# Levels three to five of the block inverse on quarters of the TensorE array

## The chip, the cores and the metric

The kernel runs on one core of a Trainium2 chip. The metric is the device time of one execution in microseconds; of several executions the median counts. TensorE (PE in the profile) multiplies matrices: a weight load (PEld) puts the stationary operand into its 128 x 128 array, and a matmul streams the moving operand past it into PSUM. A matmul whose stationary operand is smaller than the array needs only a part of it; which part follows from the partitions that its operands come from (rows) and the partitions of PSUM that it writes (columns). The trace gives this form as rows*columns, such as 128*64. VectorE (DVE), ScalarE (ACT) and GpSimd (POOL) do the elementwise work, SyncE (SP) starts most of the transfers.

## What is computed

One step of a small hybrid decoder: a first layer with windowed attention and a gated delta rule side by side, a second with a Conformer convolution. The part around the change is the delta rule, which is computed in chunks; it asks for the inverse of a unit lower triangular matrix in every chunk and head:

```python
def gated_delta_rule(q, k, v, g, beta, s0):
    ...
    lower = jnp.tril(jnp.einsum('...id,...jd->...ij', kb, kc) * decay, -1)
    a_mat = lower + jnp.eye(c, dtype=f32)
    rhs = jnp.concatenate([vc * bc[..., None], kb * jnp.exp(gcum)[..., None]], axis=-1)
    sol = lax.linalg.triangular_solve(a_mat, rhs, left_side=True, lower=True, unit_diagonal=True)
    ...
    s_fin, o = lax.scan(step, s0.astype(f32), (u, w, attn, qg, kg, g_last))
```

There are eight heads and 512 prompt tokens. The kernel takes chunks of 128 tokens, so a head has four matrices of 128 x 128 to invert. The rest is projections: 132 weight tiles of 2048 x 128 against 576 tokens (512 of the prompt, 64 sampled), 2048 channels each.

## The kernel before

**The projections.** Every weight tile and the activations are split in two parts (`w_hi`, `w_lo`, `act_hi`, `act_lo`), and `proj` (L596) does one eighth of a tile with twelve matmuls: two blocks of 128 channels, three products each, two halves of 288 tokens. The eighths are the clock of the kernel: every engine has a list by eighths (slots), written out by hand, and TensorE takes its queue strictly in the order in which it is written.

**A head in 32 slots.** `head_unit` runs through four weight tiles, 32 slots, while it does the delta rule of the head before: `PE_PLAN`, `DVE_PLAN`, `ACT_PLAN` and `POOL_PLAN` say which step stands in which slot. Steps wait for each other through counters (`pe_h`, `dve_h`, `act_h`, `pool_h`).

**The inverse.** `solve_blocks` inverts the 8 x 8 blocks on the diagonal on VectorE (L1787 is its shuffle). Then levels 3 to 6 double the size of the inverted blocks. `POOL` masks the level's part of the matrix into `mtl` (step `L{l}`). TensorE multiplies it by the inverse so far (step `a{l}`, L817, for level 6 L820), ScalarE copies the product out of PSUM (`A{l}`), TensorE multiplies the transposed inverse by that copy (step `x{l}`, L830, for level 6 L839), and VectorE subtracts the result from the inverse (`X{l}`). As the 128 x 128 matrix falls into two blocks of 64 up to level 5, the inverse is kept compactly in `x_d`: 64 columns for each chunk, its lower-right block on the upper 64 partitions and its upper-left block on the lower 64 (`lower` and `upper` are these halves of the partitions, `diagonal` is the pair of them). The transposed inverse `xt` is kept at full width, 128 x 128 for each chunk, with zeros outside the two blocks. Levels 3 and 4 make it anew by transposing `x_d` (`T{l}`, L1858; the first is made by `Xt`, and `X` transposes it into `x_d`, L1839). Level 5 updates both `x_d` and `xt`, with eight more matmuls for the second (L835).

**How the level steps use the array.** In `a` and `x` of levels 3 to 5 there are two matmuls for each of four chunks, one for each half. Each takes all 128 rows (its operands come from all partitions, half of one of them being zeros) and 64 columns. Every fp32 matmul stands in the trace as two passes, so eight matmuls are 16 rows of the trace (x16). All four chunks' results lie in one bank of PSUM: bank 1 for `a`, bank 2 for `x`, bank 3 for the second product of level 5.

Of the kernel before, what the change touches and what calls it, by code (L numbers as in the profile page):

```python
# [20 lines left out]
P = 128  # L21
# [3 lines left out]
SEQ = 512  # L25
NC = SEQ // P
NS = NB * NT
# [8 lines left out]
LEVELS, FIRST = 7, 3  # L36
# [179 lines left out]
def hybrid_step(nc, x, wt, w_ab, const, param, dn_prev, state_in, k_cache, v_cache, cf_prev,  # L216
# [3 lines left out]
    with ExitStack() as ctx:  # L220
# [57 lines left out]
        o_tok = cut(SEQ).rearrange("p (c t) -> p c t", t=P)  # L278
        a1 = cut(SEQ).rearrange("p (c t) -> p c t", t=P)
        st = cut(P)  # L280
# [15 lines left out]
        lower, upper = slice(0, HP2), slice(HP2, P)  # L296
        diagonal = (lower, upper)
        kq_sq = fa[:, 3584:4608].rearrange("p (c t) -> p c t", t=P)
        o_sq = fa[:, 4096:4608].rearrange("p (c t) -> p c t", t=P)
# [284 lines left out]
        def _(pe):  # L584
# [203 lines left out]
            def head_step(it, kb, name):  # L788
# [21 lines left out]
                elif name[0] == "a":  # L810
# [3 lines left out]
                    if l < LEVELS - 1:  # L814
                        for c in range(NC):
                            for h_ in diagonal:
                                ins = pe.matmul(gp[h_, 1, cd(c)], mtl[l % 2][:, c, h_], x_d[:, c, :], start=True, stop=True)  # L817
                    else:
                        for c, out in ((0, upper), (2, lower), (1, upper), (3, lower)):
                            ins = pe.matmul(gp[out, 1, cd(c)], mtl[l % 2][:, c, upper], x_d[:, c, :], start=True, stop=True)  # L820
                elif name[0] == "x":
# [4 lines left out]
                    if l < LEVELS - 1:  # L826
                        for c in range(NC):
                            for h_ in diagonal:
                                a_ = a1_d[:, c, :] if l in IN_BLOCKS else a1[:, c, h_]
                                ins = pe.matmul(half_blocks(gp[h_, 2, cd(c)], l, 0), xt[:, c, h_], half_blocks(a_, l, 0),  # L830
                                                start=True, stop=True)
                        if l not in IN_BLOCKS:
                            for c in range(NC):
                                for h_ in diagonal:
                                    ins = pe.matmul(half_blocks(gp[h_, 3, cd(c)], l, 1), a1[:, c, h_],  # L835
                                                    half_blocks(xt[:, c, h_], l, 1), start=True, stop=True)
                    else:
                        for c, out in ((0, lower), (2, upper), (1, lower), (3, upper)):
                            ins = pe.matmul(gp[out, 3, cd(c)], a1_d[:, c, :], xt[:, c, upper], start=True, stop=True)  # L839
                elif name == "o_chan":  # L840
# [279 lines left out]
        def _(act):  # L1120
# [69 lines left out]
            def head_act(it, kb, name):  # L1190
# [11 lines left out]
                elif name[0] == "A":  # L1202
                    l = int(name[1])
                    act.wait_ge(pe_h.sem, pe_h.at(f"a{l}", it))
                    a_ = gp[:, 1, 0:NC * HP2].rearrange("p (c t) -> p c t", t=HP2)
                    if l in IN_BLOCKS:
                        ins = copy(a1_d, a_)
                    elif l < LEVELS - 1:
                        for h_ in diagonal:
                            ins = copy(a1[h_, :, h_], a_[h_])  # L1210
                    else:
                        copy(a1_d[upper, 0:2], a_[upper, 0:2])
                        ins = copy(a1_d[upper, 2:NC], a_[lower, 2:NC])
# [315 lines left out]
        def _(dve):  # L1529
# [264 lines left out]
            def head_dve(it, kb, name):  # L1794
# [34 lines left out]
                elif name == "Xt":  # L1829
                    dve.wait_ge(dve_h.sem, dve_h.at("solve", it))  # L1830
                    ins = tt(xt.rearrange("p c (b j) -> p c b j", j=BLOCK), blocks_wide(z_h, P),
                             blocks_mask(z_h, C_BLK + P, P), MUL)
                elif name == "X":
                    if isinstance(it, int) and it == 0:
                        for h_, other in (diagonal, diagonal[::-1]):
                            dve.memset(a1[h_, :, other], 0.0)
                    dve.wait_ge(dve_h.sem, dve_h.at("Xt", it))
                    for h_ in diagonal:
                        ins = dve.transpose(x_d[h_], xt[h_, :, h_])  # L1839
                elif name[0] == "X":  # L1840
# [3 lines left out]
                    if l < LEVELS - 1:  # L1844
                        part = half_blocks(x_d.rearrange("p c t -> p (c t)"), l, 0)
                        ins = tt(part, part, half_blocks(gp[:, 2, 0:NC * HP2], l, 0), SUB)
                        if l not in IN_BLOCKS:
                            b_ = 1 << l
                            for h_ in diagonal:
                                part = xt[h_, :, h_][:, :, b_:2 * b_]  # L1850
                                ins = tt(part, part, new(3)[h_, :, b_:2 * b_], SUB)
                    else:
                        ts(xt[lower, 0:2, upper], new(3)[lower, 0:2], -1.0)
                        ins = ts(xt[lower, 2:NC, upper], new(3)[upper, 2:NC], -1.0)
                elif name[0] == "T":
                    dve.wait_ge(dve_h.sem, dve_h.at(f"X{name[1]}", it))
                    for h_ in diagonal:
                        ins = dve.transpose(xt[h_, :, h_], x_d[h_])  # L1858
                elif name[0:2] == "vp":
# [946 lines left out]
```

## Time and profile before

| | us |
|---|---|
| median of 3 runs | 1935.72 |
| lowest and highest | 1934.87, 1937.52 |
| the profiled execution | 1932.56 |
| its span, first to last instruction | 1930.7 |
| busy: PE, DVE, ACT, POOL | 1905.5, 1244.3, 713.8, 658.9 |
| granted TensorE clock, mean | 0.997 of full |

The profile's page gives for each engine its busy time, for 40 slices of the span the busy share of each engine, the waits and the chain of work that ended last. The chain that ended last is 88% TensorE, 76% on the one line of `proj`. The timeline gives the instructions of an engine in order of time, those of one kind merged, with their start, how long the merged ones took together, and their count.

### The profile page before, as it was taken

How to read it: one execution, taken by the hardware profiler on the slowest of the kernel's cores; microseconds unless marked ns; L12 is line 12 of the kernel's file. 1: busy time of each engine (PE TensorE's matmuls, PEld its weight loads, DVE VectorE, ACT ScalarE, POOL GpSimd, SP SyncE). 2: the span in 40 equal slices, each digit the busy share in tenths (PEclk: the TensorE clock that was granted, in tenths of full speed). 3: DMA queues.
4: the chain of work that ended last, by engine and by line, in shares of the span. 5: the costliest groups of instructions: out<-in, count | busy, mean ns of one | idle time of the engine just before them, and what ended most of it. 6: DMA issues, size and time to landing. Idle time of an engine off the chain costs nothing.

```text
span 1930.7 us, 37255 instructions
## 1 busy us (share of the span) xinstructions
PE 1905.5 (99%) x15516; PEld 1857.2 (96%) x15516; DVE 1244.3 (64%) x2515; ACT 713.8 (37%) x1303; POOL 658.9 (34%) x652
## 2 busy tenths in 40 slices
PE   7999999999999999999999999999999999999997
PEld 6999999999999898899999999999999999999997
DVE  6767766776654556745332689999999755473334
ACT  5322222232222135533222455555565433342220
POOL 0222322232222220003110468888888750031110
PEclk9999999999999999999999999999999999999998
DMA  6322222222223542123434334333333222233333
GB/s 203 94 73 72 73 68 73 72 74 68 68 73 117 167 161 61 55 69 124 132 118 127 93 100 98 98 82 91 97 99 89 79 88 66 88 96 121 105 107 119
DMA packets 78361, 186.31 MB, mean 96 GB/s; under 512 B 26944, under 2 KB 32000, under 8 KB 77944
## 3 DMA queue, kind: packets, MB, share of 16 engines
q1 hardware_dynamic: 70272, 166.42, 29.0%
q0 software_dynamic: 4176, 11.74, 1.9%
q10 hardware_dynamic: 3744, 5.77, 0.8%
q8 instruction: 122, 2.00, 0.4%
q14 instruction: 47, 0.39, 0.1%
HBM read 164.82 MB, written 19.08 MB: 95 GB/s over the span
## 4 chain that ended last, share of the span: by engine, by line
PE 88%; DVE 6%; POOL 2%; issue 2%; DMA 1%; ACT 1%; SPq 0%; POOLq 0%; DVEq 0%; ACTq 0%
PE acc L596 76%; POOL arena L2350 2%; PE acc L674 2%; DVE full L1542 1%; DVE w_lo L1539 1%; DVE act_lo L1539 1%; DVE gp L1542 1%; PE gp L817 1%; PE gp L830 1%; PE gp L808 1%; PE gp L965 1%; PE gp L978 1%; PE gp L986 1%; DMA w_raw<-wt 1%; DVE arena L1539 1%
## 5 line engine op out<-in xcount | busy, mean ns | idle before, releaser
L596 PE MATMUL acc<-act_hi,w_hi 128*128 128x288 f32 x3936 | 864.6, 301 | 3.4 <-DVE w_lo L1539 3.1
L596 PE MATMUL acc<-act_hi,w_lo 128*128 128x288 f32 x3936 | 841.8, 295 | 0.0
L596 PE MATMUL acc<-act_lo,w_hi 128*128 128x288 f32 x3936 | 841.0, 295 | 0.0
L596 PEld LDWEIGHTS acc<-act_hi,w_hi 128*128 128x128 f32 x3936 | 629.8, 189 | 20.7 <-issue 12.1
L596 PEld LDWEIGHTS acc<-act_hi,w_lo 128*128 128x128 f32 x3936 | 633.1, 189 | 0.0
L596 PEld LDWEIGHTS acc<-act_lo,w_hi 128*128 128x128 f32 x3936 | 632.2, 188 | 0.0
L2350 POOL TENSOR_TENSOR arena<-arena 128x512 f32<-128x512 f32 (+1 forms) x268 | 377.6, 1409 | 338.4 <-ACT arena L1385 278.3
L1122 ACT ACTIVATE w_hi<-w_raw 128x1024 fp32r<-128x1024 f32 x264 | 277.3, 1058 | 419.8 <-PE acc L596 294.4
L1539 DVE TENSOR_TENSOR w_lo<-w_raw,w_hi 128x1024 fp32r<-128x1024 f32 x264 | 373.4, 1434 | 40.8 <-ACT w_hi L1122 39.9
L1542 DVE SCALAR_TENSOR_TENSOR gp<-arena,par,gp 128x64 f32<-128x64 f32 (+1 forms) x688 | 248.0, 441 | 0.0
L1122 ACT ACTIVATE arena<-arena,par 128x512 f32<-128x512 f32 x240 | 165.2, 720 | 103.8 <-POOL arena L2350 91.9
L1539 DVE TENSOR_TENSOR full<-acc,arena 128x576 f32<-128x576 f32 (+3 forms) x52 | 36.8, 708 | 229.8 <-PE acc L596 211.9
L2350 POOL TENSOR_TENSOR small<-small 128x4 f32<-128x4 f32 (+3 forms) x95 | 55.0, 584 | 189.6 <-DVE small L1547 73.5
L2350 POOL TENSOR_TENSOR arena<-arena,cst 128x24 f32<-128x24 f32 (+4 forms) x93 | 30.2, 342 | 254.9 <-DVE arena L1539 127.9
L2350 POOL TENSOR_TENSOR full<-full,cst 128x512 f32<-128x512 f32 x40 | 69.4, 1745 | 79.8 <-DVE full L1839 46.2
L2350 POOL TENSOR_TENSOR act_lo<-full,act_hi 128x576 fp32r<-128x576 f32 (+1 forms) x32 | 43.9, 1392 | 145.5 <-ACT act_hi L1122 145.4
L1542 DVE SCALAR_TENSOR_TENSOR arena<-arena,small 128x512 f32<-128x512 f32 (+2 forms) x145 | 74.4, 559 | 0.5
L1542 DVE SCALAR_TENSOR_TENSOR arena<-arena,acc 128x576 f32<-128x576 f32 x24 | 18.0, 750 | 81.2 <-ACT arena L1478 74.2
L1122 ACT ACTIVATE full<-gp 128x256 f32<-128x256 f32 (+1 forms) x48 | 16.5, 343 | 142.8 <-PE gp L817 115.0
L1122 ACT ACTIVATE arena<-gp,small 128x128 f32<-128x128 f32 x28 | 10.3, 367 | 151.6 <-PE gp L855 107.0
L1122 ACT ACTIVATE arena<-gp 128x512 f32<-128x512 f32 (+4 forms) x50 | 26.3, 552 | 98.4 <-PE gp L978 36.3
L1539 DVE TENSOR_TENSOR full<-full,gp 128x576 f32<-128x576 f32 (+2 forms) x72 | 32.7, 488 | 31.8 <-PE gp L835 22.7
(270 smaller groups left out, 1687.0 us busy)
## 6 DMA issues: line engine op xcount, KB each, us to landing
w_raw<-wt SPq DMA_DIRECT2D x264, 512.0 KB, 4.0
full<-x SPq DMA_DIRECT2D x8, 576.0 KB, 9.1
arena<-x SPq DMA_DIRECT2D x16, 288.0 KB, 3.6
arena<-x_scratch SPq DMA_DIRECT2D x16, 288.0 KB, 2.9
x_scratch<-full ACTq DMA_DIRECT2D x14, 288.0 KB, 4.0
arena<-state_in SPq DMA_DIRECT2D x6, 512.0 KB, 5.1
out_sdn<-arena POOLq DMA_DIRECT2D x6, 512.0 KB, 3.1
out_y<-full SPq DMA_DIRECT2D x16, 160.0 KB, 1.9
```

What stands on the lines that cost most here:

```text
L596: ins = pe.matmul(acc[:, s, i, 0:HALF], w[:, s, wk], a[:, k, i * HALF:(i + 1) * HALF], start=(k == 0 and j == 0), stop=(k == KT - 1 and j ...
L674: ins = pe.matmul(acc[:, s, a, 0:part_width(a, n >= N_OUT1)], w[:, s, wk], x_[:, k, part(a, n >= N_OUT1)], start=(k == 0 and j == 0), stop ...
L808: ins = pe.matmul(gp[:, 2 + c // 2, (c % 2) * 256:(c % 2) * 256 + 256], kt[:, ck(c)], kqv[kb][:, 0:2, ck(c)], start=True, stop=True)
L817: ins = pe.matmul(gp[h_, 1, cd(c)], mtl[l % 2][:, c, h_], x_d[:, c, :], start=True, stop=True)
L830: ins = pe.matmul(half_blocks(gp[h_, 2, cd(c)], l, 0), xt[:, c, h_], half_blocks(a_, l, 0), start=True, stop=True)
L965: ins = pe.matmul(gp[:, q, j * 256 + w * P:j * 256 + (w + 1) * P], full[rows, 4 * r + 2 * jj + j, blk(c):blk(c) + P], kv[rows, 2 * r, blk( ...
L978: ins = pe.transpose(gp[:, 2 + w, g * P:(g + 1) * P], prob[u % 2][:, g, w * P:(w + 1) * P], ident)
L986: ins = pe.matmul(gp[64 * q:64 * q + 64, 2, 0:256], v_tok[:, c - 1 + w, r, 64 * q:64 * q + 64], probT[:, w, 2 * q:2 * q + 2, :], start=(w ...
L1122: return act.activation(out, in_, ACT.Copy, scale=scale)
L1539: return dve.tensor_tensor(out, a, b, op)
L1542: return dve.scalar_tensor_tensor(out=out, in0=a, scalar=scalar, in1=b, op0=op0, op1=op1)
L2350: return pool.tensor_tensor(out, a, b, op)
```

## The change

The transposed inverse of levels 3 to 5 becomes compact too: a new tile `xt_d` of 64 columns for each chunk takes the place of `a1`. For chunks 0 and 1 (`straight`) it lies on the same half of the partitions as `x_d`, for chunks 2 and 3 (`crossed`) on the other half; `turned_home` gives the half. All matmuls of levels 3 to 5 take operands from 64 partitions. The results of chunks 2 and 3 go to a second bank, and the chunks are taken in the order 0, 2, 1, 3. The copy `A{l}` reads two banks, and is one instruction for level 5 as well. On VectorE `Xt`, `X` and `T{l}` are three instructions each (chunks 0 and 1, then each half of chunks 2 and 3), and `X5` writes the full-width `xt` with four subtractions, from the second product of level 5, which is now computed at full width (64 columns). Level 6 works on the full `xt` as before, with 64 rows instead of 128 in its second step.

```diff
         o_tok = cut(SEQ).rearrange("p (c t) -> p c t", t=P)
-        a1 = cut(SEQ).rearrange("p (c t) -> p c t", t=P)
+        xt_d = cut(SEQ)[:, 0:SEQ // 2].rearrange("p (c t) -> p c t", t=HP2)
         st = cut(P)
...
         diagonal = (lower, upper)
+        straight, crossed = slice(0, NC // 2), slice(NC // 2, NC)
+
+        def turned_home(half, c):
+
+            return half if c < NC // 2 else diagonal[half == lower]
         kq_sq = fa[:, 3584:4608].rearrange("p (c t) -> p c t", t=P)
...
                     if l < LEVELS - 1:
-                        for c in range(NC):
+                        for c in (0, 2, 1, 3):
                             for h_ in diagonal:
-                                ins = pe.matmul(gp[h_, 1, cd(c)], mtl[l % 2][:, c, h_], x_d[:, c, :], start=True, stop=True)
+                                ins = pe.matmul(gp[turned_home(h_, c), c // 2, cd(c % 2)], mtl[l % 2][h_, c, h_], x_d[h_, c, :],
+                                                start=True, stop=True)
                     else:
...
                     if l < LEVELS - 1:
-                        for c in range(NC):
+                        for c in (0, 2, 1, 3):
                             for h_ in diagonal:
-                                a_ = a1_d[:, c, :] if l in IN_BLOCKS else a1[:, c, h_]
-                                ins = pe.matmul(half_blocks(gp[h_, 2, cd(c)], l, 0), xt[:, c, h_], half_blocks(a_, l, 0),
-                                                start=True, stop=True)
+                                r_ = turned_home(h_, c)
+                                ins = pe.matmul(half_blocks(gp[h_, 2 + c // 2, cd(c % 2)], l, 0), xt_d[r_, c, :],
+                                                half_blocks(a1_d[r_, c, :], l, 0), start=True, stop=True)
                         if l not in IN_BLOCKS:
                             for c in range(NC):
-                                for h_ in diagonal:
-                                    ins = pe.matmul(half_blocks(gp[h_, 3, cd(c)], l, 1), a1[:, c, h_],
-                                                    half_blocks(xt[:, c, h_], l, 1), start=True, stop=True)
+                                for r_ in diagonal:
+                                    ins = pe.matmul(gp[r_, 2, cd(4 + c)], a1_d[r_, c, :], xt_d[r_, c, :], start=True, stop=True)
                     else:
                         for c, out in ((0, lower), (2, upper), (1, lower), (3, upper)):
-                            ins = pe.matmul(gp[out, 3, cd(c)], a1_d[:, c, :], xt[:, c, upper], start=True, stop=True)
+                            ins = pe.matmul(gp[out, 3, cd(c)], a1_d[upper, c, :], xt[upper, c, upper], start=True, stop=True)
                 elif name == "o_chan":
...
                     a_ = gp[:, 1, 0:NC * HP2].rearrange("p (c t) -> p c t", t=HP2)
-                    if l in IN_BLOCKS:
-                        ins = copy(a1_d, a_)
-                    elif l < LEVELS - 1:
-                        for h_ in diagonal:
-                            ins = copy(a1[h_, :, h_], a_[h_])
+                    if l < LEVELS - 1:
+                        ins = copy(a1_d.rearrange("p (b c) t -> p b (c t)", b=2), gp[:, 0:2, 0:P])
                     else:
...
                     dve.wait_ge(dve_h.sem, dve_h.at("solve", it))
-                    ins = tt(xt.rearrange("p c (b j) -> p c b j", j=BLOCK), blocks_wide(z_h, P),
-                             blocks_mask(z_h, C_BLK + P, P), MUL)
+                    wide = xt_d.rearrange("p c (b j) -> p c b j", j=BLOCK)
+                    for h_, chunks in ((slice(0, P), straight), (lower, crossed), (upper, crossed)):
+                        z = z_h[h_, chunks]
+                        ins = tt(wide[h_ if chunks == straight else diagonal[h_ == lower], chunks], blocks_wide(z, HP2),
+                                 blocks_mask(z, C_BLKM, NS)[h_], MUL)
                 elif name == "X":
                     if isinstance(it, int) and it == 0:
-                        for h_, other in (diagonal, diagonal[::-1]):
-                            dve.memset(a1[h_, :, other], 0.0)
+                        dve.memset(xt[upper, :, lower], 0.0)
                     dve.wait_ge(dve_h.sem, dve_h.at("Xt", it))
-                    for h_ in diagonal:
-                        ins = dve.transpose(x_d[h_], xt[h_, :, h_])
+                    dve.transpose(x_d[:, straight], xt_d[:, straight])
+                    for h_, r_ in (diagonal, diagonal[::-1]):
+                        ins = dve.transpose(x_d[h_, crossed], xt_d[r_, crossed])
                 elif name[0] == "X":
...
                     if l < LEVELS - 1:
-                        part = half_blocks(x_d.rearrange("p c t -> p (c t)"), l, 0)
-                        ins = tt(part, part, half_blocks(gp[:, 2, 0:NC * HP2], l, 0), SUB)
+                        halved = lambda ap: ap.rearrange("p s (n a b) -> p s n a b", a=2, b=1 << l)[:, :, :, 0, :]
+                        part = halved(x_d.rearrange("p (s c) t -> p s (c t)", s=2))
+                        ins = tt(part, part, halved(gp[:, 2:4, 0:P]), SUB)
                         if l not in IN_BLOCKS:
-                            b_ = 1 << l
+                            new_t = gp[:, 2, NC * HP2:2 * NC * HP2].rearrange("p (c t) -> p c t", t=HP2)
                             for h_ in diagonal:
-                                part = xt[h_, :, h_][:, :, b_:2 * b_]
-                                ins = tt(part, part, new(3)[h_, :, b_:2 * b_], SUB)
+                                for chunks, r_ in ((straight, h_), (crossed, diagonal[h_ == lower])):
+                                    ins = tt(xt[h_, chunks, h_], xt_d[r_, chunks], new_t[r_, chunks], SUB)
                     else:
...
                     dve.wait_ge(dve_h.sem, dve_h.at(f"X{name[1]}", it))
-                    for h_ in diagonal:
-                        ins = dve.transpose(xt[h_, :, h_], x_d[h_])
+                    dve.transpose(xt_d[:, straight], x_d[:, straight])
+                    for h_, r_ in (diagonal, diagonal[::-1]):
+                        ins = dve.transpose(xt_d[r_, crossed], x_d[h_, crossed])
                 elif name[0:2] == "vp":
```

On TensorE the order around level five of a head is, before and then in the changed kernel (shapes are those of the outputs):

```order
L596 MATMUL acc<-act_hi,w_lo 128x288 x2
L817 MATMUL gp<-full 64x64 x8
L596 MATMUL acc<-act_hi,w_hi 128x288 x2
...
L596 MATMUL acc<-act_hi,w_lo 128x288 x2
L830 MATMUL gp<-arena,full 64x32 x8
L835 MATMUL gp<-full,arena 64x32 x8
L596 MATMUL acc<-act_hi,w_hi 128x288 x2
```

```order
L601 MATMUL acc<-act_hi,w_lo 128x288 x2
L822 MATMUL gp<-full 64x64 x8
L601 MATMUL acc<-act_hi,w_hi 128x288 x2
...
L601 MATMUL acc<-act_hi,w_lo 128x288 x2
L836 MATMUL gp<-full,arena 64x32 x8
L841 MATMUL gp<-arena,full 64x64 x8
L601 MATMUL acc<-act_hi,w_hi 128x288 x2
```

The number of matmuls and their place between the projection's matmuls are the same; the second product of level five has 64 columns instead of 32.

On VectorE, between the solving of the 8 x 8 blocks and the next split of weights (`w_lo`), and after level five's x step, before:

```order
L1539 TENSOR_TENSOR full<-arena,cst 128x512
L1839 STREAM_TRANSPOSE full<-full 64x256 x2
L1539 TENSOR_TENSOR w_lo<-w_raw,w_hi 128x1024
...
L1539 TENSOR_TENSOR full<-full,gp 128x4x32
L1539 TENSOR_TENSOR full<-full,gp 64x4x32 x2
L1542 SCALAR_TENSOR_TENSOR arena<-arena 128x512
```

and in the changed kernel:

```order
L1541 TENSOR_TENSOR arena<-arena,cst 128x128
L1541 TENSOR_TENSOR arena<-arena,cst 64x128 x2
L1842 STREAM_TRANSPOSE full<-arena 128x128
L1844 STREAM_TRANSPOSE full<-arena 64x128 x2
L1541 TENSOR_TENSOR w_lo<-w_raw,w_hi 128x1024
...
L1541 TENSOR_TENSOR full<-full,gp 128x4x32
L1541 TENSOR_TENSOR full<-arena,gp 64x2x64 x4
L1544 SCALAR_TENSOR_TENSOR arena<-arena 128x512
```

Three instructions become six at the start, three become five after level five, and no step changes its place in the order.

## Rows read from the trace of the kernel before

**Rows 1.** The stretch of the second head: busy time of each engine, clock, DMA

```profile
core 0: us, PE busy (x) PEld busy (x) DVE busy (x) ACT busy (x) POOL busy (x), PEclk, DMA share, GB/s
162.60:227.47 64.87, 64.87 (x573) 62.89 (x572) 45.68 (x114) 18.11 (x49) 18.32 (x29) 1.00 0.23 71
```

**Rows 2.** The waits of TensorE over the whole span, the two longest

```profile
engine line waited for: us in total, times, longest us
PE acc L738 <- ACT act_hi L1122: 8.9, 2, 8.7
PE acc L596 <- DVE w_lo L1539: 3.1, 4, 1.7
```

**Rows 3.** The timeline of TensorE: levels three and five of the second head

```profile
start us, us, engine line op out<-in xcount [idle before <-releaser]
162.60 0.69 PE L817 MATMUL gp<-full 128*64 128x64 f32 x16
163.22 0.53 PE L596 MATMUL acc<-act_hi,w_hi 128*128 128x288 f32 x2
...
165.00 0.66 PE L830 MATMUL gp<-full 128*64 128x32 f32 x16
165.59 0.53 PE L596 MATMUL acc<-act_hi,w_hi 128*128 128x288 f32 x2
...
172.14 0.69 PE L817 MATMUL gp<-full 128*64 128x64 f32 x16
...
174.53 0.66 PE L830 MATMUL gp<-arena,full 128*64 128x32 f32 x16
...
175.59 0.53 PE L596 MATMUL acc<-act_hi,w_hi 128*128 128x288 f32 x2
```

**Rows 4.** The timeline of TensorE: level six of the second head, half as many matmuls

```profile
177.38 0.45 PE L820 MATMUL gp<-full 128*64 128x64 f32 x8
177.76 0.53 PE L596 MATMUL acc<-act_hi,w_hi 128*128 128x288 f32 x2
```

**Rows 5.** The timeline of TensorE: sampled state, four column positions at once

```profile
621.46 0.30 PE L921 MATMUL gp<-full,arena 128*32 128x128 f32 x2
621.47 0.30 PE L921 MATMUL gp<-arena 128*32 128x128 f32 x2
...
623.34 0.53 PE L596 MATMUL acc<-act_hi,w_hi 128*128 128x288 f32 x2
```

**Rows 6.** The timeline of TensorE: matmuls of 64 rows in the sampled steps

```profile
606.60 0.68 PE L909 MATMUL gp<-cst,arena 64*64 64x64 f32 x16
607.21 0.54 PE L596 MATMUL acc<-act_hi,w_hi 128*128 128x288 f32 x2
...
828.94 0.44 PE L1002 MATMUL gp<-arena 64*32 64x128 f32 x8
...
831.37 0.53 PE L596 MATMUL acc<-act_hi,w_hi 128*128 128x288 f32 x2
```

**Rows 7.** The timeline of VectorE: the start of the inverse, second head

```profile
156.30 0.19 DVE L1539 TENSOR_TENSOR arena<-cst,arena 128x32 f32<-128x32 f32 x1
...
160.33 0.69 DVE L1539 TENSOR_TENSOR full<-arena,cst 128x512 f32<-128x512 f32 x1
161.06 0.89 DVE L1839 STREAM_TRANSPOSE full<-full 64x256 f32<-64x256 f32 x2
```

**Rows 8.** The timeline of VectorE: after the x steps of levels four and five

```profile
170.85 0.27 DVE L1539 TENSOR_TENSOR full<-full,gp 128x128 f32<-128x128 f32 x1
...
175.71 0.78 DVE L1539 TENSOR_TENSOR full<-full,gp 128x128 f32<-128x128 f32 x3 [2.67 <-PE gp L835]
```

**Rows 9.** The timeline of VectorE and TensorE: the start of the inverse, first head

```profile
96.04 0.64 DVE L1836 MEMSET arena<- 64x256 f32 x2
96.69 0.89 DVE L1839 STREAM_TRANSPOSE full<-full 64x256 f32<-64x256 f32 x2
...
97.72 0.69 PE L817 MATMUL gp<-full 128*64 128x64 f32 x16
```

## The prediction

> **What bounds the kernel now.** I read the granted clock first: it is full in the heads [rows 1], so the clock explains nothing. Then the busy time of one head, from its first `a3` to that of the next: TensorE is busy in 64.87 of 64.87 us, VectorE in 45.68, and the others in less than 19 [rows 1]. Then the waits of TensorE: they come to 16 us in the whole execution, the longest is at the start of the kernel, and none is at a step of a head [rows 2]. TensorE works through its queue in the written order. So what a step takes on TensorE, from its first matmul to the next one of the projection, is on the path that sets the end, and a microsecond taken from it is a microsecond of the kernel, as long as nothing on another engine comes too late. The other engines matter only through that. Last, the timeline of TensorE and VectorE around the steps that change.
>
> The eight heads are alike within some hundredths of a us, but for the first (VectorE is later there) and the last (VectorE has less to do). I work it out for the second and multiply by eight.
>
> **What a step takes.** `a3` holds TensorE for 163.22 - 162.60 = 0.62 us, with 16 passes, and `x3` for 165.59 - 165.00 = 0.59, with 16 passes of 32 columns [rows 3]. `x5` with both its products has 32 passes and takes 175.59 - 174.53 = 1.06 [rows 3]. `a6` has the same form as `a3` and half the passes, and takes 177.76 - 177.38 = 0.38 [rows 4]. So eight more passes cost 0.62 - 0.38 = 0.24 us, and eight passes more with 32 columns cost (1.06 - 0.59) / 16 x 8 = 0.235: the number of columns streamed does not matter at this size. The rest of `a6`, 0.38 - 0.24 = 0.14, is what a step costs once, whatever it holds.
>
> Now 0.24 us for eight passes is 0.03 for each. Are they one after the other, or two at a time with 0.06 for each pair? The step of the sampled state has 64 passes of 128 columns in 623.34 - 621.46 = 1.88 us, 0.029 for each, although its columns are twice as many; its matmuls take a quarter of the array's columns and go to four places in turn, and the second pair starts 0.01 after the first [rows 5]. So places of the array work at the same time: four at a time, a round of four takes about 0.11 with 128 columns. In the changed steps today there are two places, the two halves of the columns, and a round of two takes 0.06.
>
> **Part 1, `a3`, `a4`, `a5`, `x3`, `x4`: four places instead of two.** The matmuls are as many as before, eight for each product. They now take 64 rows each, and the order of chunks 0, 2, 1, 3 puts four in a row on the four different quarters: both halves straight, then both crossed. If the four run together, 16 passes are four rounds instead of eight, and four rounds of 0.06 go: 0.24. I give back 0.02 since the second pair starts a little later [rows 5]. That is 0.22 us for each of the five steps, 1.10 for a head. The rounds themselves should not get shorter: nothing in them is smaller but the rows, and a step of matmuls of 64 rows takes 607.21 - 606.60 = 0.61 for 16 passes, as `a3` does with 128 [rows 6]. That also prices the change of form at the edges of a step: nothing.
>
> Do quarters of both kinds run together? The nearest row is the step of the sampled attention: 64 passes of 128 columns and 64 of 8, on four places that lie in both halves of the rows and in all four quarters of the columns, from 828.94 to 831.37, 2.43 us, 0.019 for each [rows 6]. One place alone has 16 passes of each kind; with 0.11 for a pass of 128 columns they are 1.76 us, and so 2.43 leaves no room for two places in turn, which would be 3.5 and more. This is the end that I take. The other end is no gain from rows at all, eight rounds as before: the saving is then 0. No row of this trace has the very case, two row halves on the same columns in turn with two column halves on the same rows.
>
> **Part 2, `x5`.** Its first product gains 0.22 like the others. Its second product has 64 columns instead of 32, straight quarters only for all chunks, since all four land on their own half of the partitions: eight rounds as before. By `a3` against `x3`, 64 columns for 32 cost 0.62 - 0.59 = 0.03 in a step. So `x5` gains 0.19. `a6` and `x6` keep two places at a time: 0.
>
> **The sum on TensorE:** 5 x 0.22 + 0.19 = 1.29 us for a head, 8 heads: 10.3 us.
>
> **Part 3, VectorE, off the path unless it comes late.** `Xt` was one multiplication of 128x512 for 0.69; one of 128x32 takes 0.19 [rows 7], so a column costs 0.50/480, and one of 128 columns about 0.29. Three are 0.87: 0.18 more. `X` was two transposes of 256 columns, 0.89 together [rows 7]; one of 128 columns is between 0.22 (half) and 0.445 (no cheaper), I take 0.445 - 128 x 0.50/480 = 0.31, so three are 0.93: 0.04 more. `X` ends at 161.95 and `a3` starts at 162.60 [rows 3, 7], so 0.65 us cover 0.22. In the first head `X` ends at 97.58 for an `a3` at 97.72 [rows 9], 0.14, but there one of two memsets of 0.64 goes, 0.32: cover 0.46 for 0.22. At the dear end of the transposes (three of 0.445) `X` costs 0.44 more, and the first head waits 0.16 once.
>
> `X5` was three subtractions for 0.78 [rows 8] and is five of the same 128 columns, so 0.78 x 5/3 = 1.30. It starts when `x5` ends, at 175.71, and `a6` needs it at 177.38 [rows 4, 8]: of 1.67 us, 0.89 were free and 0.37 still are. `X4` ends at 171.12 and `a5` follows at 172.14 [rows 3, 8]; two steps before it shrink by 0.44 together, which leaves 0.58, less 0.04 for the transposes of `T3`. `T3` and `T4` cost 0.04 more each. In all VectorE gets 0.18 + 3 x 0.04 + 0.52 = 0.82 us more for each head, against the 19 that it had free [rows 1].
>
> **Part 4, ScalarE and GpSimd.** The copies `A3`, `A4` read as many elements from two banks, and `A5` becomes one instruction from two; each starts when its `a` step ends, and the way on TensorE from there to the `x` step is untouched. GpSimd's masks are unchanged, and `L4` starts 0.22 later than now at most. No queue gets a new wait.
>
> **The rivals.**
>
> *Pairs only (chance 0.09).* The quarters run two at a time as the halves did. For it: no row shows four quarters of 64x64. Against it: the sampled attention above. TensorE then gains nothing and `x5` pays 8 x 0.03 = 0.2: 1935.9.
>
> *A bank shared by two row halves (0.05), slower.* The straight quarters write one bank from both halves of the rows. If such a pair must go in turn, the first eight matmuls of a step still find a partner in the other bank, and stay at eight rounds; but the second product of `x5` has all eight matmuls in one bank, and its 8 rounds become 16: 8 x 0.06 = 0.48 more for a head, 3.8 in all, with the 0.2 above 1939.7. Against it: the step at 606.60 writes bank 0 from both row halves and takes 0.61 for 16 passes, not the 1.1 that they would take in turn [rows 6]. The Trainium skill (TensorEngine Tiling (Array Packing), Restrictions and Gotchas) states just this rule: that different row tiles cannot access the same PSUM bank simultaneously. By that rule the time is this rival's; the trace disagrees.
>
> *Going between straight and crossed empties the array (0.04), far slower.* Each step changes three times within eight matmuls; at the price of a step's fixed part, 0.14, that is 0.42 against the 0.22 gained, so 0.20 more for each of 48 products: 1935.7 + 9.6 = 1945.3. It decides against the change from 0.07 us for each passage. Against it: the two forms of the sampled attention change place with every matmul, at 0.019 a pass [rows 6].
>
> *VectorE late (0.07).* If a subtraction from the two tiles costs as much as 0.445, `X5` takes 2.1 us and `a6` waits 0.4, 8 x 0.4 = 3.2 back: 1928.6.
>
> *The quarters overlap, but less than fully (0.07),* three at a time or with a longer first round: half of the gain, 1930.5.
>
> **How the numbers follow.** The likeliest case is the full sum, with chance 0.68. The profiled execution took 1932.56 (span 1930.7, and 1.9 around it); less 10.3 it is 1922.3. The median lies 3.2 above the profiled execution; 1935.72 - 10.3 = 1925.4 is my forecast for it. The lower end: without the 0.02 and 0.03 that I gave back, the gain is 8 x 6 x 0.24 = 11.5, and the three runs start 0.9 under their median: 1923. The upper end takes in late VectorE and the half gain: 1930.5. Within 0.2% (3.9 us, about what a measurement of this kernel can tell from no change) falls the case of pairs, and above it the two slower ones. Faster by over 0.2%: 0.68 + 0.07 + 0.07 = 0.82; same 0.09; slower 0.05 + 0.04 = 0.09. The range leaves out these last two cases and the one of pairs, 0.18.
>
> **What would show it.** `a3` to the next matmul of the projection at 0.40 instead of 0.62, `x3` at 0.37 instead of 0.59, `x5` at 0.87 instead of 1.06; a head of 63.6 us instead of 64.87; no wait of TensorE for VectorE at `a3` or `a6`; the first pass of four matmuls starting within 0.03 us. If `a3` still takes 0.62, quarters don't run together and I am wrong at the root; if it takes 0.40 and a head is not 1.3 us shorter, something waits that I took for covered, `X5` first.

## The result

| | kernel before | changed kernel |
|---|---|---|
| median, us | 1936.14 (5 runs) | 1926.11 (5 runs) |
| lowest, highest | 1934.87, 1938.56 | 1921.80, 1929.88 |
| the profiled execution | 1932.56, span 1930.7 | 1927.03, span 1925.2 |

The ratio is 0.9949, with an interval from 0.9934 to 0.9964: 10.0 us faster, and by that interval anything from 7.0 to 12.8 us. The forecast was 1925.4, from 1923.0 to 1930.5. In a second comparison on another occasion the same kernel had 1924.99 against 1936.81, ratio 0.9943 (0.9930 to 0.9956).

A head, the row that answers to [rows 1] (columns as there; from the first `a3` of the second head to that of the third), in the changed kernel:

```profile
core 0: us, PE busy (x) PEld busy (x) DVE busy (x) ACT busy (x) POOL busy (x), PEclk, DMA share, GB/s
161.81:225.41 63.60, 63.60 (x574) 61.62 (x573) 46.79 (x121) 17.76 (x48) 18.13 (x29) 1.00 0.24 73
```

It is 1.27 us shorter, 63.60 for 64.87, and TensorE is still busy in all of it. The heads after it measure the same, in this profile and in the second one of the changed kernel; the first came out at 63.61 and 63.49. VectorE works 1.1 us more, ScalarE 0.35 less. Times eight that is 10.2 us.

The timeline of TensorE in the changed kernel, for the steps of [rows 3, 4] (start, duration of the merged instructions, line, form, count):

```profile
161.81 0.46 PE L822 MATMUL gp<-full 64*64 64x64 f32 x16
162.20 0.53 PE L601 MATMUL acc<-act_hi,w_hi 128*128 128x288 f32 x2
...
163.99 0.43 PE L836 MATMUL gp<-full,arena 64*64 64x32 f32 x16
164.35 0.40 PE L601 MATMUL acc<-act_hi,w_hi 128*128 128x288 f32 x1
...
172.65 0.43 PE L836 MATMUL gp<-full,arena 64*64 64x32 f32 x16
172.91 0.66 PE L841 MATMUL gp<-arena,full 64*64 64x64 f32 x16
173.50 0.53 PE L601 MATMUL acc<-act_hi,w_hi 128*128 128x288 f32 x2
...
175.29 0.45 PE L826 MATMUL gp<-full 128*64 128x64 f32 x8
175.67 0.40 PE L601 MATMUL acc<-act_hi,w_hi 128*128 128x288 f32 x1
```

The form is now 64*64. From the first matmul to the next one of the projection `a3` takes 0.39 instead of 0.62 us, `x3` 0.36 instead of 0.59, `x5` 173.50 - 172.65 = 0.85 instead of 1.06. `a6`, which the change leaves alone, takes 0.38 as before. How many passes are under way in the first 0.03 us of `a3`, in the kernel before and in the changed one (this line's matmuls and then its weight loads, busy time and count):

```profile
162.60:162.63 0.03, 0.03 (x2) 0.03 (x2) 1.00 0.00 0
161.81:161.84 0.03, 0.03 (x4) 0.03 (x4) 1.00 0.00 0
```

Two have started in the one and four in the other, by 0.02 us after the first; in both kernels the next ones follow 0.06 us apart, from the second round on. Within `x5` the first product, in quarters, holds TensorE for 0.26, and the second, with as many passes but on straight quarters alone, for 0.59.

The timeline of VectorE at the start of the inverse and after level five, against [rows 7, 8]:

```profile
159.55 0.89 DVE L1541 TENSOR_TENSOR arena<-arena,cst 128x128 f32<-128x128 f32 x3
160.48 0.31 DVE L1842 STREAM_TRANSPOSE full<-arena 128x128 f32<-128x128 f32 x1
160.80 0.63 DVE L1844 STREAM_TRANSPOSE full<-arena 64x128 f32<-64x128 f32 x2
...
173.62 0.29 DVE L1541 TENSOR_TENSOR full<-full,gp 128x128 f32<-128x128 f32 x1 [1.50 <-PE gp L841]
173.82 1.17 DVE L1541 TENSOR_TENSOR full<-arena,gp 64x128 f32<-64x128 f32 x4
175.03 0.83 DVE L1544 SCALAR_TENSOR_TENSOR arena<-arena 128x512 f32<-128x512 f32 x2
```

`X` ends at 161.43, 0.38 before `a3`; `X5` ends at 174.99, 0.30 before `a6`. Both had more room before (0.65 and 0.89), and neither stops TensorE now.

The waits of TensorE, against [rows 2]:

```profile
PE acc L743 <- ACT act_hi L1127: 9.0, 3, 8.7
PE acc L601 <- DVE arena L1544: 7.6, 1, 7.6
PE acc L601 <- DVE w_lo L1541: 4.0, 5, 1.7
```

There is one new wait, of 7.6 us, and it is not in the heads: it stands at 1518 us, at the end of the convolution part. The profiled execution is only 5.5 us shorter than the one of before, although its heads are 10.2 shorter. What the wait is, and what part it has in that, was to be found out.

### The profile page after: what moved, and what is told of

It reads as the page before. It is cut to its first block, busy times and chain, and to the rows that moved or that the text cites. A ratio compares the mean times of both kernels' runs of the same rounds, so it can differ in the third digit from the quotient of the medians.

```text
span 1925.2 us, 37302 instructions
## 1 busy us (share of the span) xinstructions
PE 1891.6 (98%) x15516; PEld 1842.8 (96%) x15516; DVE 1265.5 (66%) x2570; ACT 709.7 (37%) x1295; POOL 667.5 (35%) x652
## 4 chain that ended last, share of the span: by engine, by line
PE 72%; POOL 16%; DVE 6%; issue 4%; ACT 1%; DMA 1%; POOLq 0%; SPq 0%; DVEq 0%; ACTq 0%
PE acc L601 61%; POOL arena L2357 15%; PE acc L679 2%; DVE full L1544 2%; DVE act_lo L1541 1%; DVE arena L1541 1%; DVE w_lo L1541 1%; DVE gp L1544 1%; PE gp L813 1%; PE gp L970 1%; PE gp L983 1%; PE gp L991 1%; POOL out_cfs L2641 1%; DMA full<-x 1%; PE gp L822 0%
## 5 line engine op out<-in xcount | busy, mean ns | idle before, releaser
L2357 POOL TENSOR_TENSOR arena<-arena 128x512 f32<-128x512 f32 (+1 forms) x268 | 385.6, 1439 | 334.6 <-ACT arena L1387 283.9
L1541 DVE TENSOR_TENSOR w_lo<-w_raw,w_hi 128x1024 fp32r<-128x1024 f32 x264 | 386.8, 1488 | 27.9 <-ACT w_hi L1127 27.0
L1127 ACT ACTIVATE arena<-gp,small 128x128 f32<-128x128 f32 x28 | 10.3, 368 | 151.2 <-PE gp L860 107.1
L1127 ACT ACTIVATE arena<-gp 128x512 f32<-128x512 f32 (+3 forms) x34 | 20.2, 634 | 63.3 <-PE gp L983 36.4
L1127 ACT ACTIVATE act_hi<-full 128x576 fp32r<-128x576 f32 (+1 forms) x64 | 32.6, 557 | 26.3 <-DVE full L1544 25.7
```

The lines of the kernel that those rows point to most:

```text
L1127: return act.activation(out, in_, ACT.Copy, scale=scale)
L1541: return dve.tensor_tensor(out, a, b, op)
L2357: return pool.tensor_tensor(out, a, b, op)
```

## The experiments

**The order of the chunks.** The edit, in both first products:

```diff
-                        for c in (0, 2, 1, 3):
+                        for c in range(NC):
```

> The changed kernel with one edit: in the first product of levels three to five the chunks are taken in the order 0, 1, 2, 3, so that two straight chunks come first and then two crossed ones. Same matmuls, same quarters, same banks. Theory (the gain comes from four quarters at work together, and TensorE's queue finds the partners that stand next to each other): most of it goes, since the crossed quarters can start only when the second straight pair has started; seven rounds instead of four, a3 to the next projection matmul 0.57 us instead of 0.39, and a head 6 x 0.18 = 1.1 us longer, 64.7 instead of 63.6. Rival (TensorE looks far enough ahead to find the crossed matmuls behind the second straight pair): a3 stays at 0.39 to 0.42. Second rival (the gain comes from the 64 rows, not from the quarters): no change either, 0.39.

`a3` in the timeline of TensorE:

```profile
160.93 0.47 PE L822 MATMUL gp<-full 64*64 64x64 f32 x16
161.34 0.53 PE L601 MATMUL acc<-act_hi,w_hi 128*128 128x288 f32 x2
```

0.41 us (to the nanosecond 0.405, against 0.392 in the order 0, 2, 1, 3), and a head is 63.67 instead of 63.60 us. The first theory's forecast of 0.57 was wrong, the rival's 0.39 to 0.42 right: in the written order the crossed matmuls would have to wait behind the second straight pair, for seven rounds in all, and the step is too short for that. So within a step TensorE doesn't keep strictly to the written order, as the section on the kernel before has it. The order written into the change is worth 0.07 us for a head: 0.013 in each of `a3`, `a4`, `a5`, `x3` and `x4`, nothing in `x5`. This run alone doesn't tell quarters from rows; the one with the rows alone does. (One execution: 1925.96.)

**How far the queue looks.** The same place, with both matmuls of a quarter next to each other, so that every second matmul finds its place taken by the one before it, and the last quarter's first matmul stands seventh of eight:

```diff
-                        for c in (0, 2, 1, 3):
-                            for h_ in diagonal:
+                        for half, c in ((0, 0), (0, 1), (1, 0), (1, 1), (0, 2), (0, 3), (1, 2), (1, 3)):
+                            for h_ in (diagonal[half],):
```

> The changed kernel with the first product of levels three to five ordered by quarters: both matmuls of one quarter next to each other, then both of the next. With the order 0, 1, 2, 3 the step lost only 0.013 us, so TensorE's queue finds a free quarter behind at least two matmuls that must wait. Theory (the queue looks over all eight): a3 to the next matmul at 0.39 to 0.43 us. Rival (it looks over a few only): each quarter starts when the one before it has its second matmul under way, about seven rounds, 0.55 us.

```profile
161.66 0.48 PE L822 MATMUL gp<-full 64*64 64x64 f32 x16
162.07 0.53 PE L601 MATMUL acc<-act_hi,w_hi 128*128 128x288 f32 x2
```

0.41 us again, and a head of 63.71. Within a step of eight matmuls the order hardly matters; the seventh still starts in the first round. What the orders do cost shows in the starts of the four passes of the first round: 0, 7, 14 and 20 ns in the changed kernel, 0, 7, 27 and 34 with the order 0, 1, 2, 3, and 0, 13, 27 and 40 here. The last of the four comes 14 and 20 ns later, and the steps are 13 and 20 ns longer (0.405 and 0.412 for 0.392). (One execution: 1927.03.)

**The rows alone.** The kernel before, with operands from 64 partitions and everything else where it was:

```diff
-ins = pe.matmul(gp[h_, 1, cd(c)], mtl[l % 2][:, c, h_], x_d[:, c, :], start=True, stop=True)
+ins = pe.matmul(gp[h_, 1, cd(c)], mtl[l % 2][h_, c, h_], x_d[h_, c, :], start=True, stop=True)
...
-                                a_ = a1_d[:, c, :] if l in IN_BLOCKS else a1[:, c, h_]
+                                a_ = a1_d[h_, c, :] if l in IN_BLOCKS else a1[h_, c, h_]
```

and so for `xt` and for the second product.

> The kernel before with one edit: the matmuls of levels three to five take their operands from the 64 partitions that hold anything but zeros, for all chunks in place (straight quarters only, no crossing, nothing else moved). Theory (quarters): nothing changes on TensorE, a3 0.62, x3 0.59, x5 1.06 us, a head 64.87 us. Rival (half the rows make a pass cheaper, whatever the quarter): a3 near 0.39 and a head near 63.6 us as in the changed kernel.

`a3` and `x5` in the timeline of TensorE:

```profile
163.60 0.68 PE L817 MATMUL gp<-full 64*64 64x64 f32 x16
164.21 0.53 PE L596 MATMUL acc<-act_hi,w_hi 128*128 128x288 f32 x2
...
175.54 0.66 PE L830 MATMUL gp<-arena,full 64*64 64x32 f32 x16
176.03 0.63 PE L835 MATMUL gp<-full,arena 64*64 64x32 f32 x16
176.59 0.53 PE L596 MATMUL acc<-act_hi,w_hi 128*128 128x288 f32 x2
```

The form is 64*64, as in the changed kernel, and the steps take 0.61 and 1.05 us, as before; a head is 64.89. So fewer rows are worth nothing by themselves. The gain comes with the crossed chunks, which use the two quarters that lay idle. They also bring a second bank for the results, and straight quarters alone with two banks were not run; what speaks against the bank stands with the rivals. (One execution: 1937.61.)

**Both products of level five in quarters.** The change left the second product on straight quarters. Here its results for chunks 2 and 3 come out on their home half in the next bank:

```diff
-                                    ins = pe.matmul(gp[r_, 2, cd(4 + c)], a1_d[r_, c, :], xt_d[r_, c, :], start=True, stop=True)
+                                    ins = pe.matmul(gp[turned_home(r_, c), 2 + c // 2, cd(4 + c % 2)], a1_d[r_, c, :], xt_d[r_, c, :],
+                                                    start=True, stop=True)
...
-                                    ins = tt(xt[h_, chunks, h_], xt_d[r_, chunks], new_t[r_, chunks], SUB)
+                                    ins = tt(xt[h_, chunks, h_], xt_d[r_, chunks], new_t(s)[h_], SUB)
```

with the chunks in the order 0, 2, 1, 3 there too, and `new_t(s)` the part of bank 2 or 3.

> The changed kernel with the second product of level five in quarters as well: the chunks in the order 0, 2, 1, 3, the results of chunks 2 and 3 come out on their home half in the next bank, and X5 subtracts them from xt_d on the other half. Theory (any product gains by four quarters): eight rounds become four, x5 takes 0.84 - 0.22 = 0.62 us instead of 0.84, a head 63.38 instead of 63.60, the kernel 1.8 us faster than the changed one, 0.9940 of the kernel before. Rival (a subtraction whose two inputs lie on different partitions is dearer, or the second product is held up by the first): a6 waits or x5 stays at 0.84, no gain.

```profile
172.11 0.43 PE L836 MATMUL gp<-full,arena 64*64 64x32 f32 x16
172.36 0.44 PE L841 MATMUL gp<-arena,full 64*64 64x64 f32 x16
172.74 0.53 PE L601 MATMUL acc<-act_hi,w_hi 128*128 128x288 f32 x2
```

The second product takes 172.74 - 172.36 = 0.38 instead of 0.59, and `x5` 0.63. A head:

```profile
224.64:288.02 63.38, 63.38 (x573) 61.40 (x572) 46.63 (x121) 17.76 (x48) 18.66 (x29) 1.00 0.24 73
```

63.38, as expected, and the four subtractions, of which the two for the crossed chunks now have their inputs on different halves, cost what they did (1.18 us together). The whole: median 1923.17 (1922.39 to 1925.77), ratio to the kernel before 0.9940 (0.9926 to 0.9953). This product, too, goes to two banks now.

**VectorE's cover.** Four more subtractions in `X5`, into memory that nothing reads:

```diff
+                                    tt(idle[h_, chunks], xt_d[r_, chunks], new_t[r_, chunks], SUB)
                                     ins = tt(xt[h_, chunks, h_], xt_d[r_, chunks], new_t[r_, chunks], SUB)
```

> The changed kernel with four more subtractions of 64x128 in X5, from the same tiles into memory that nothing reads, one before each of its own. A dose for the cover of X5. In the changed kernel X5 ends 0.29 us before a6 starts. Four more at about 0.27 are 1.1 us. Theory (X5 is covered by 0.29 and no more): a6 starts about 0.8 us late in each head, a head is 64.4 instead of 63.6 us, and the kernel 6 to 7 us slower than the changed one. Rival (there is more room than the timeline shows, since VectorE's queue drains before): a head stays at 63.6 us.

The waits of TensorE, and `X5`'s first and last subtraction with the `a6` that follows:

```profile
PE gp L828 <- DVE full L1543: 4.8, 8, 0.6
```

```profile
173.27 0.29 DVE L1543 TENSOR_TENSOR full<-full,gp 128x128 f32<-128x128 f32 x1 [1.64 <-PE gp L843]
...
175.19 0.27 DVE L1543 TENSOR_TENSOR full<-arena,gp 64x128 f32<-64x128 f32 x1
```

```profile
175.60 0.45 PE L828 MATMUL gp<-full 128*64 128x64 f32 x8 [0.61 <-DVE full L1543]
```

`X5` takes 2.19 us for 1.37, so the four cost 0.82, about 0.2 each and less than the 1.1 I counted with at 0.27 each. `a6` comes late in all eight heads, by 0.6, and a head is 64.24 instead of 63.60, 0.64 more. Eight times 0.64 are 5.1 us, where I expected 6 to 7. The cover was thus real and small, 0.82 - 0.64 = 0.18; the timeline's 0.30 before `a6` is not all of it free, since TensorE starts `a6` 0.14 after `X5`'s end at the earliest (175.46 to 175.60). By this one dose the changed kernel stands some 0.2 us in each head from a new wait. (One execution: 1930.46.)

**What the new wait is.** The changed kernel and the one with both products in quarters once more, beside each other, and the kernel before.

> The changed kernel once more, beside the one below on the same chip. By the sum of the steps, 8 x 1.27 = 10.2 us less than the kernel before, whatever the rest of the execution does: ratio 0.9947. A head is 63.60 us in every execution. Theory on the spread of its runs (8 us, where the kernel before has 4): it is not the heads; where the matmuls of the projection follow each other at 0.130 instead of 0.133 us in the convolution part, VectorE and GpSimd don't follow and TensorE waits some 7 us at its end, so that the faster pace there brings nothing. Then this profile shows either both (the faster pace between 1150 and 1450, and the wait of 7.6 us) or neither. Rival: the wait comes from the change and shows in every profile of it.

> The kernel with both products of level five in quarters again, against the changed kernel of this call. By the steps it is 8 x 0.22 = 1.8 us faster than the changed one. Rival: its 1923.2 against 1926.1 was the state of the rest of the execution, and the two agree within 1 us.

> The kernel before once more, for one more profile. Theory: a head is 64.87 us again, a3 takes 0.62; and if its matmuls follow at 0.130 us in the convolution part, it too has a wait of several us for VectorE at the end of that part. Rival: only the changed kernel has that wait.

The stretch from 1200 to 1300 us, in the middle of the convolution part, where TensorE does nothing but the projection: the first profile of the changed kernel, then the second, then the second of the kernel before, then the second of the kernel with both products in quarters.

```profile
1200.00:1300.00 100.00, 100.00 (x771) 100.00 (x771) 96.92 (x220) 57.38 (x78) 89.30 (x67) 1.00 0.36 95
```

```profile
1200.00:1300.00 100.00, 100.00 (x753) 100.00 (x752) 93.74 (x217) 56.70 (x77) 86.88 (x68) 1.00 0.35 91
```

```profile
1200.00:1300.00 100.00, 100.00 (x753) 100.00 (x752) 93.92 (x217) 57.65 (x78) 86.60 (x67) 1.00 0.35 94
```

```profile
1200.00:1300.00 100.00, 100.00 (x771) 100.00 (x771) 96.92 (x215) 58.21 (x79) 89.23 (x68) 1.00 0.35 90
```

At the same granted clock of 1.00, 771 matmuls in one execution and 753 in another, 0.130 and 0.133 us each. The first profile of the changed kernel and the second with both products in quarters have the faster pace, and both have the wait; in the second profile of the changed kernel neither is there. The waits of that profile, whole down to 1.7 us, and then that of the second one with both products in quarters:

```profile
PE acc L743 <- ACT act_hi L1127: 8.3, 3, 8.0
PE acc L601 <- DVE w_lo L1541: 2.7, 3, 1.7
```

```profile
PE acc L743 <- ACT act_hi L1128: 8.3, 1, 8.3
PE acc L601 <- DVE arena L1545: 7.5, 1, 7.5
```

So the wait isn't there in every execution of the changed kernel, as the rival had it; it goes with the pace. Of ten profiles three have the faster pace there, and these three (`order_0123` is the third) have the wait of 7.5 to 7.6 us; the seven others have at most 0.6 at that place. At the faster pace VectorE is busy 96.9% of the stretch, against 93.7 at the slower. My reading, which no run tests, is that VectorE is then at its limit, that TensorE runs ahead until its two buffers are full, and that the time comes back in one piece. Around the wait the granted clock is low for some microseconds (0.91 in the mean of 1490 to 1530 in the first profile of the changed kernel, 1.00 in the second). All in all the convolution part is not shorter at the faster pace but longer: from the 9600th matmul in the trace to the 12650th it takes 408.7 us in the first profile and 406.8 in the second; in the first profile of the kernel before it takes 407.0. What could not be tested is the kernel before at that pace in that part: none of its three profiles (the one with 64 rows is the third) had it, so that it would have the same wait is not shown.

The two times of this comparison: 1924.99 (1923.77 to 1927.70) for the changed kernel, 1924.48 (1923.80 to 1925.37) with both products in quarters, ratio 0.9939 (0.9925 to 0.9954). By the steps 1.8 us were expected between them; 0.5 was measured here, 2.9 between the first two sets of runs, and both sets spread by more. In the trace `x5` and the head are shorter by 0.22 us in both profiles of it; in the medians the 1.8 us are not settled.

## Why the prediction was right

**What bounds the kernel.** Right. A microsecond off a head's steps on TensorE is one off the head: read to the nanosecond, the steps lose 3 x 0.224 + 2 x 0.224 + 0.210 = 1.33, and the head loses 1.27, 0.02 less than forecast. Of the 0.06 between, 0.035 come back in front of the level steps, where the projection's matmuls before them take up to 0.01 more, and 0.025 in the stretch between `x6` and the step that follows it. Why is open; the prediction had put the edges of a step at nothing.

**Four places at a time.** Right, and borne out three times: the rows alone bring nothing, the change with its crossed quarters 0.22 us for a product, and a second product put on them gains the same again. The step of the sampled attention, with four places over both halves of the rows, was the row to trust [rows 6]. The fourth pass of a step starts 0.02 us after the first, where 0.03 was the sign that I had named. Of the terms, `a3` came out at 0.39 (forecast 0.40), `x3` at 0.36 (0.37), `x5` at 0.85 (0.87). I took the order of the chunks for what makes the four meet. That reason was wrong: with other orders the step loses 0.01 to 0.02.

**64 columns instead of 32.** I gave back 0.03 for the second product of `x5`. Its eight rounds took 0.59 us; the same eight with 32 columns, in the run with rows alone, 176.59 - 176.03 = 0.56. The 0.03 is there.

**VectorE.** `Xt` 0.89 (forecast 0.87), `X` 0.95 (0.93), `X5` 1.37 (1.30). In all VectorE works 1.1 us more for a head where 0.82 was forecast. The cover at `a3` was 0.38 (forecast 0.43), at `a6` 0.30 (0.37). No wait came, but by the dose some 0.2 us more would have brought one, 8 times.

**The rivals.** Pairs only: fell, by 0.39 against 0.62. A bank shared by two row halves: fell. The straight pair writes bank 0 from both row halves and the crossed pair bank 1, and sixteen passes take four rounds; with turns in each bank they would take eight. In the run with the rows alone `a3` has all eight matmuls in one bank from both row halves, and the second product of `x5` in the changed kernel likewise: they took 0.61 and 0.59 and not the 1.1 that turns would need. So for results on different partitions of a bank the Trainium skill's rule (TensorEngine Tiling (Array Packing), Restrictions and Gotchas) that different row tiles can't access one bank at the same time is not what these runs show. Whether it holds for two row halves that write the same partitions of one bank was not tried: the change keeps them in different banks. An empty array between straight and crossed: fell, with every order. VectorE late: fell, the four subtractions from the two tiles took 1.17 and not the 1.78 of 0.445 each. Less than full overlap: fell, with 0.39 for a forecast of 0.40.

A rival that I did not list is the second bank: that the results of a step go faster when they are spread over two. No run has straight quarters alone with two banks. Against it stands the step of the sampled state in the kernel before [rows 5]: by its source the first four matmuls all write bank 0, on four places, and they start within 0.02 us of each other. So four places meet in one bank too. That two banks bring nothing on two places is argued by this and not shown.

**The time of the whole.** 10.0 us by the medians against 10.3 forecast. That these agree to 0.3 us is luck, since the interval of the measured gain is 7.0 to 12.8 us; what bears the forecast out is the 10.2 us of the heads. That the first profiles differ by 5.5 only comes of the rest of the two executions. Up to the 9600th matmul the changed kernel is 9.9 us ahead. In the convolution part, with its faster pace and its wait, it loses 1.7. Behind that it gains 1.6, since in the execution of before the granted clock fell (0.91 in the mean of 1580 to 1600 us, 1.00 in the changed kernel's). In the last 200 us, where TensorE is busy all but throughout, it loses 4.3, since there the execution of before had the faster pace. The rows of 1800 to 1900, before and changed:

```profile
1800.00:1900.00 100.00, 100.00 (x763) 100.00 (x762) 34.69 (x25) 20.97 (x24) 12.25 (x9) 1.00 0.33 98
```

```profile
1800.00:1900.00 100.00, 100.00 (x745) 100.00 (x743) 30.97 (x23) 19.84 (x23) 10.90 (x8) 1.00 0.30 91
```

The second profiles of both kernels, neither with the faster pace anywhere after 1100 us, have spans of 1934.2 and 1922.0: 12.2 us. 10.2 of it are the heads, 0.9 lie ahead of them, at the start, and 0.7 in the convolution part, where the kernel before waited for VectorE for 0.6 in this execution; the last 0.4 are spread.

## What to carry to other kernels

Small matmuls that come in batches, here of eight in fp32 with up to 64 columns and operands that fill half of the rows, gained when they were spread over all quarters of the array; taking fewer rows in place brought nothing. Results of the two row halves on the same partitions went to different banks here, and one bank for them was not tried. If half of the matmuls keep their data on the other half of the partitions, the moves between the halves can be had from copies, transposes and subtractions that are made anyway: here for 1.1 us more of VectorE in a head, which stayed covered with 0.2 us to spare. And before a gain of half a per cent is read from one pair of profiles, compare stretches: here the heads said 10.2 us while the two spans said 5.5.

## What the runs showed that I had not expected

- The projection's matmuls follow each other at 0.133 us or at 0.130 us at the same granted clock of 1.00, for stretches of hundreds of microseconds, in either kernel: 753 or 771 in 100 us. It moves an execution by about 4 us where TensorE is the limit (the last 200 us, from the 14000th matmul to the last, take 200.9 us in the first profile of the kernel before and 205.2 in the second), and to the worse, by 1.7 us, in the convolution part, where VectorE is busy 96.9% of the time. What sets it is open.
- TensorE starts a matmul for a free quarter ahead of others that must wait, up to the seventh of the eight of a step: 0.39, 0.41 and 0.41 us in three orders. The orders differ by how late the fourth quarter's first pass starts, 20, 34 and 40 ns after the first.
- A round of two places and one of four cost the same, 0.06 us for up to 64 columns: the second product of `x5` has sixteen passes, in 0.59 us on two places and in 0.38 on four.
- A subtraction of 64x128 whose input in PSUM lies on the other half of the partitions than its input in SBUF costs the same as one with both on the same half: four, two of them of this kind, took 1.18 us, and four with both on the same half 1.17.
